# The last block's second FF product by Strassen's seven products, in a Trainium2 kernel of a hybrid decoder layer

## The chip, the cores and the metric

One core of one Trainium2 chip. The metric is the device time of one execution, in microseconds. The kernel before takes 2714.3 us, the median of three runs (2713.03 to 2716.78).

## What is computed

One decoder layer for 2048 tokens of width 1024, in float32, cut here to what matters:

```python
z = rms_norm(x, norm_mix_g) @ w_in
mixed = concatenate([rwkv7_heads(z), window_attention(z)])
x = x + mixed @ w_out
u = rms_norm(x, norm_mlp_g)
x = x + square(relu(u @ w_ff_up)) @ w_ff_down        # 1024 -> 4096 -> 1024
e = rms_norm(p @ ple_proj, ple_norm_g)
x = x + e * sigmoid(x @ ple_gate)
return rms_norm(x, final_norm_g)
```

The change concerns `square(relu(u @ w_ff_up)) @ w_ff_down` for the last 512 tokens.

## The kernel before

**Blocks and stages.** The tokens go in four blocks of 512 (TBK), b = 0 to 3. A block passes through `norm` and `proj` (input projection), `mix` (four tiles of 128 tokens, 26 steps each: the delta rule and the attention) and `fin` (output projection, norm, FF, the embedding branch ple and its gate, final norm). Each of the five engines runs the same `whole_program`: first the blocks' projections with the mixing of block 0 beside them, then `fin(b - 1)` beside the mixing of block b, where two hand-written lists of places (`BESIDE_PROJ`, `BESIDE_FIN`) say after how many pieces of `fin` each mixing step stands in the engine's order. `fin(3)`, the last, runs alone. The order on an engine is fixed; engines wait for each other by semaphores, one count for each step named in the lists `FIN_PE`, `FIN_ACT`, `FIN_DVE` (class `Marks`). The queues of SP (all loads of weights) and GpSimd run in order too; GpSimd has no work.

**Precision.** A product a x w is made of three matmuls in fp32r: a_hi x w_hi, a_hi x w_lo, a_lo x w_hi, where hi is the number rounded to fp32r and lo the rest.

**Weights.** They pass in chunks of 128 x 1024 numbers (512 KB), numbered over the whole kernel. SP loads chunk n into `raw`, slot n % 4, once the low part of chunk n - 4 is written (`load_weights`, L377). ScalarE copies it into `w_hi` (`high`, L980), VectorE writes `w_lo` (`low`, L1292) and TensorE begins the chunk when that is done. `w_hi` and `w_lo` have two slots: chunk n + 1 is split while chunk n is multiplied.

**FF.** The hidden width of 4096 goes in four groups (g, HG = 4) of 1024. The up product of a group has eight steps i, one chunk of 24 matmuls each (`up_half`, L860 to L864), whose result of 128 hidden features x 512 tokens lies in one of PSUM's banks 0 to 3. VectorE makes relu and the token's scale into `tmp` (L1636), ScalarE squares it twice, as h_hi (L1172) and exactly (L1173), VectorE writes the rest h_lo (L1639). In block 3's program ScalarE and VectorE split the next weight chunk ahead of each step's relu. The down product of a group has two column halves n of four chunks c, in which four token tiles j are multiplied in banks 0 to 3 (`by_tokens`, L818, L821, L822), 24 matmuls a chunk; VectorE adds the four banks into x (L1655) after each half: 8 adds a group. In the last group, eight transposes of the p block (L907, "pt") stand between up and down in banks 0 and 1; ScalarE and VectorE take them as p_hi (L1178) and p_lo (L1645), and the group's first down matmuls wait for p_lo. The row of scales comes from TensorE to `stage_f` by ScalarE (L1170, inv_row); after the FF `e_copy` (L1195) writes the ple product to the same memory `e`.

```python
for k in range(2):                                             # by_tokens, token tile j
    mm = T.matmul(ps[:, j, :], ah, wh, start=(first and k == 0), stop=False)
    T.matmul(ps[:, j, :], ah, wl, start=False, stop=False)
    mm = T.matmul(ps[:, j, :], al, wh, start=False, stop=(final and k == 1))
```

Of the kernel before, what the change touches and what calls it, by code (L numbers as in the profile page):

```python
# [13 lines left out]
P = 128  # L14
# [7 lines left out]
ZT = 20  # L22
# [84 lines left out]
class Marks:  # L107


    def __init__(self, sem, steps):  # L110
        self.sem, self.steps, self.seen = sem, steps, 0
        self.place = {s: i for i, s in enumerate(steps)}
        assert len(self.place) == len(steps)

    def mark(self, step):
        assert self.steps[self.seen % len(self.steps)] == step, (self.steps[self.seen % len(self.steps)], step)
        self.seen += 1
        return self.sem

    def done(self, n, step):  # L120
        return self.sem, n * len(self.steps) + self.place[step] + 1
# [58 lines left out]
FIN_CHUNKS = 8 + HG * 16 + 2 + 8  # L180

# [56 lines left out]
def finish_layer(nc, x, p, mixT, out, params, consts, ple_g, final_g, w_out, w_up, w_down, w_ple, w_gate, first_block):  # L238
# [3 lines left out]
    with ExitStack() as ctx:  # L242
# [20 lines left out]

        ones = sb("ones", [P, P])
# [30 lines left out]
        attT = pp[:, 0, :, :]  # L295

# [35 lines left out]
        fin_pe, fin_act, fin_dve = Marks(sem("fin_pe"), FIN_PE), Marks(sem("fin_act"), FIN_ACT), Marks(sem("fin_dve"), FIN_DVE)  # L332
# [7 lines left out]
        LAST_CHUNK = fin_chunk(BLOCKS - 1, FIN_CHUNKS - 1)  # L340

        def weights(n):
# [4 lines left out]
            i = (n - BLOCKS * ZT) % FIN_CHUNKS  # L347
# [4 lines left out]
            if i < HG * 16:  # L352
                g, i = divmod(i, 16)
# [4 lines left out]
            i -= HG * 16  # L358
# [6 lines left out]
        with nc.Block() as block:  # L365
            @block.sync
            def _(sp):
                def load_weights(n):
                    if n > LAST_CHUNK:
                        return  # L370
                    if n >= 4:
                        sp.wait_ge(w_lo_done, n - 3)
                    parts = weights(n)
# [94 lines left out]
                def fin(b):  # L468
# [25 lines left out]
                    for g in range(HG):  # L494
                        for i in range(8):
                            chunk()
                            yield
                            yield
                        if g == HG - 1:
# [41 lines left out]
            def _(pe):  # L541
# [3 lines left out]
                def begin(n):  # L545
# [5 lines left out]
                    return n % 2  # L551
# [252 lines left out]
                def fin(b):  # L804
# [8 lines left out]
                    def by_tokens(s, hi, lo, k0, j, first, final, name, opens):  # L813

                        for k in range(2):
                            ah, al = (a[:, k0 + k, j * P:(j + 1) * P] for a in (hi, lo))
                            wh, wl = (w[:, s, k * 512:(k + 1) * 512] for w in (w_hi, w_lo))
# [15 lines left out]

                    for n in range(2):
# [19 lines left out]
                    def up_half(s, g, i, half):  # L854
                        bank = up_bank(g, i)
                        for k in range(4 * half, 4 * half + 4):
                            if g == 0 and i == 0:
                                done(fin_dve, f"lo{k if half else 3}")
                            wh, wl = (w[:, s, k * P:(k + 1) * P] for w in (w_hi, w_lo))
# [8 lines left out]
                    for r in range(4):  # L868
# [12 lines left out]
                        yield  # L881
                    for g in range(HG):
                        for i in range(8):
# [3 lines left out]
                            elif g and i < 4:  # L887
                                done(fin_dve, f"down_add{g - 1}_1_{i}")
                            elif i >= 4:
                                done(fin_dve, f"relu{g}_{i - 4}")  # L890
# [10 lines left out]
                        if g == HG - 1:  # L901
                            pe.wait_ge(p_in, 16 * (b + 1))
                            done(fin_dve, f"relu{g}_4")
                            done(fin_dve, f"relu{g}_5")
# [878 lines left out]
```

## Time and profile before

| | us |
|---|---|
| median of three runs | 2714.3 |
| lowest and highest run | 2713.03, 2716.78 |
| span of the profiled execution, first to last instruction | 2710.3 |
| TensorE, VectorE, ScalarE, GpSimd busy in it | 2670.7, 1761.8, 1098.8, 0.2 |
| FF of the last block (about 2295 to 2640), TensorE busy | 342.5 of 345 |

The profiled execution's own device time was not kept apart from its span; beside the median of the runs the span is 4.0 us shorter. PE is TensorE's matmul, PEld its weight load, DVE VectorE, ACT ScalarE, POOL GpSimd, SP the queue that issues the loads. L1292 is line 1292 of the kernel. "Idle before" is the time that the engine stood idle just ahead of the instruction, and what ended it. Matmuls are pipelined: their durations overlap, so their starts say more than their lengths.

### The profile page before, as it was taken

Reading aid. Unit: us, or ns where it says so; the run is one execution under the profiler, and the core shown is the slowest. Engines: PE = TensorE matmul, PEld = TensorE weight load, DVE = VectorE, ACT = ScalarE, POOL = GpSimd, SP = SyncE. Lnnn points to the kernel's source line nnn. Section 1 sums busy time; section 2 is a strip of 40 time slices with the busy share of each in tenths; the row PEclk is TensorE's granted clock in tenths of the full one; section 3 lists DMA queues with packets and bytes.
Section 4 is the critical chain, followed back from the end, with each engine's and each line's share of the span. In section 5 each row is a group of like instructions: output and inputs, shape, how many; then the busy total and the mean of one; then the engine's idle time right before and its main releaser. Section 6 shows DMA issues by size and latency. Waiting matters only on the chain.

```text
span 2710.3 us, 57626 instructions
## 1 busy us (share of the span) xinstructions
PE 2670.7 (99%) x25202; PEld 2164.3 (80%) x25202; DVE 1761.8 (65%) x3037; ACT 1098.8 (41%) x1862; POOL 0.2 (0%) x4
## 2 busy tenths in 40 slices
PE   8999999999999999999999999999999999999998
PEld 6877787787878878878788888787878888888876
DVE  5477887857767674776776756867767565344435
ACT  4354444345333433653344325543434254233225
POOL 0000000000000000000000000000000000000000
PEclk9999999999999999999999999999999999999999
DMA  6564544463333334342332334433332244333332
GB/s 198 152 175 137 154 133 123 130 209 95 93 95 115 90 103 130 132 134 83 109 110 87 107 102 145 149 91 107 94 96 83 90 136 156 101 97 98 93 101 78
DMA packets 376199, 319.16 MB, mean 118 GB/s; under 512 B 48747, under 2 KB 328460, under 8 KB 375948
## 3 DMA queue, kind: packets, MB, share of 16 engines
q1 hardware_dynamic: 372272, 312.63, 38.4%
q8 instruction: 199, 3.26, 0.5%
q10 hardware_dynamic: 3676, 2.84, 0.4%
q14 instruction: 52, 0.43, 0.0%
HBM read 277.65 MB, written 38.14 MB: 117 GB/s over the span
## 4 chain that ended last, share of the span: by engine, by line
PE 79%; ACT 1%; DVE 1%; issue 0%; ACTq 0%
PE ps L818 14%; PE ps L821 13%; PE ps L822 13%; PE ps L860 9%; PE ps L864 9%; PE ps L863 9%; PE ps L703 2%; PE ps L675 1%; PE ps L831 1%; PE ps L774 1%; PE ps L622 1%; PE ps L591 1%; PE ps L614 1%; PE ps L595 1%; PE ps L594 1%; PE ps L628 1%
## 5 line engine op out<-in xcount | busy, mean ns | idle before, releaser
L1292 DVE TENSOR_TENSOR w_lo<-wraw_f,w_hi 128x1024 fp32r<-128x1024 f32 x408 | 497.5, 1219 | 345.8 <-ACT w_hi L980 344.5
L980 ACT ACTIVATE w_hi<-wraw_f 128x1024 fp32r<-128x1024 f32 x408 | 430.2, 1054 | 593.2 <-PE ps L818 504.6
L818 PE MATMUL ps<-w_hi,h_hi 128*128 128x512 f32 x1280 | 509.4, 398 | 3.1 <-DVE act_lo L1645 3.1
L821 PE MATMUL ps<-w_lo,h_hi 128*128 128x512 f32 x1280 | 499.1, 390 | 0.0
L822 PE MATMUL ps<-w_hi,h_lo 128*128 128x512 f32 x1280 | 499.0, 390 | 0.0
L860 PE MATMUL ps<-act_hi,w_hi 128*128 128x512 f32 x1024 | 412.6, 403 | 1.5 <-DVE w_lo L1292 1.4
L864 PE MATMUL ps<-act_hi,w_lo 128*128 128x512 f32 x1024 | 399.4, 390 | 0.0
L863 PE MATMUL ps<-act_lo,w_hi 128*128 128x512 f32 x1024 | 399.3, 390 | 0.0
L1172 ACT ACTIVATE h_hi<-tmp 128x512 fp32r<-128x512 f32 x128 | 80.9, 632 | 511.3 <-DVE tmp L1636 511.3
L818 PEld LDWEIGHTS ps<-w_hi,h_hi 128*128 128x128 f32 x1280 | 240.2, 188 | 58.1 <-issue 8.8
L822 PEld LDWEIGHTS ps<-w_hi,h_lo 128*128 128x128 f32 x1280 | 240.3, 188 | 51.7
L821 PEld LDWEIGHTS ps<-w_lo,h_hi 128*128 128x128 f32 x1280 | 240.5, 188 | 47.0
L860 PEld LDWEIGHTS ps<-act_hi,w_hi 128*128 128x128 f32 x1024 | 192.0, 188 | 47.1 <-issue 4.1
L864 PEld LDWEIGHTS ps<-act_hi,w_lo 128*128 128x128 f32 x1024 | 192.2, 188 | 41.6
L863 PEld LDWEIGHTS ps<-act_lo,w_hi 128*128 128x128 f32 x1024 | 192.4, 188 | 36.3
L1639 DVE TENSOR_TENSOR h_lo<-tmp,h_hi 128x512 fp32r<-128x512 f32 x128 | 88.7, 693 | 156.0 <-ACT tmp L1173 156.0
L1636 DVE SCALAR_TENSOR_TENSOR tmp<-ps,stage_f 128x512 f32<-128x512 f32 x128 | 88.3, 690 | 122.2 <-PE ps L864 119.5
L591 PE MATMUL ps<-act_hi,w_hi 128*128 128x512 f32 x320 | 129.5, 405 | 4.8 <-DVE w_lo L1292 4.4
L591 PE MATMUL ps<-h_hi,w_hi 128*128 128x512 f32 x320 | 128.6, 402 | 0.5 <-DVE h_lo L1303 0.5
L818 PE MATMUL ps<-w_hi,act_hi 128*128 128x512 f32 x320 | 126.3, 395 | 0.1
L595 PE MATMUL ps<-act_hi,w_lo 128*128 128x512 f32 x320 | 125.6, 392 | 0.0
L594 PE MATMUL ps<-act_lo,w_hi 128*128 128x512 f32 x320 | 125.4, 392 | 0.0
(227 smaller groups left out, 3731.1 us busy)
## 6 DMA issues: line engine op xcount, KB each, us to landing
wraw_f<-in_w_ff_up SPq DMA_DIRECT2D x256, 256.0 KB, 3.3
wraw_f<-in_w_ff_down SPq DMA_DIRECT2D x128, 512.0 KB, 4.0
wraw_f<-in_w_in SPq DMA_DIRECT2D x80, 512.0 KB, 4.4
zT<-tmp SPq DMA_DIRECT2D x80, 256.0 KB, 2.1
wraw_f<-in_w_out SPq DMA_DIRECT2D x32, 512.0 KB, 4.2
wraw_f<-in_w_gate SPq DMA_DIRECT2D x32, 512.0 KB, 3.9
zs<-zT SPq DMA_DIRECT2D x16, 896.0 KB, 5.8
h_lo<-mixT SPq DMA_DIRECT2D x4, 2048.0 KB, 8.8
```

What stands on the lines that cost most here:

```text
L591: mm = T.matmul(dst, wh, hi[:, k, :], start=(k == 0), stop=False)
L594: T.matmul(dst, wh, lo[:, k, :], start=False, stop=False)
L595: mm = T.matmul(dst, wl, hi[:, k, :], start=False, stop=(k == DK - 1))
L818: mm = T.matmul(ps[:, j, :], ah, wh, start=(first and k == 0), stop=False)
L821: T.matmul(ps[:, j, :], ah, wl, start=False, stop=False)
L822: mm = T.matmul(ps[:, j, :], al, wh, start=False, stop=(final and k == 1))
L860: mm = T.matmul(ps[:, bank, :], wh, act_hi[:, k, :], start=(k == 0), stop=False)
L863: T.matmul(ps[:, bank, :], wh, act_lo[:, k, :], start=False, stop=False)
L864: mm = T.matmul(ps[:, bank, :], wl, act_hi[:, k, :], start=False, stop=(k == DK - 1))
L980: S.activation(w_hi[:, n % 2, :], raw[:, n % 4, :], ACT.Copy).then_inc(w_hi_done, 1)
L1292: V.tensor_tensor(w_lo[:, n % 2, :], raw[:, n % 4, :], w_hi[:, n % 2, :].bitcast(F32), ALU.subtract).then_inc(w_lo_done, 1)
L1639: V.tensor_tensor(h_lo[:, i, :], tmp[:, i % 2, :], h_hi[:, i, :].bitcast(F32), ALU.subtract).then_inc(fin_dve.mark(f"h_lo{g}_{i}"), 1)
```

## The change

In `fin(3)` alone, the down product of each group, h (512 tokens x 1024) by w (1024 x 1024), is cut in 2 x 2 parts and made of seven products instead of eight (Strassen's, in Winograd's form). A token half is 256 wide, a feature half 512, a column half 512.

- **Factors of h.** A11, A12 and A22 are parts of h; S1 to S4 are sums of parts. The up steps go in the order 0, 4, 1, 5, 2, 6, 3, 7, so that both feature halves of a pair stand near each other. VectorE and ScalarE make of each step: for i below 4, A11 hi and lo, S3 exact, hi, lo; for i of 4 and more, A12 and A22 hi and lo, S1, S2, S4 exact, hi, lo. In this part the next weight chunk's split stands behind the step's relu and squares (ScalarE) and behind its relu (VectorE), and a step's low parts of sums stand in the following step.
- **Factors of w.** Three products take parts of w_down; four take sums, which GpSimd makes once, during the FF of block 0: 16 rounds (group, feature tile) of a load of four parts (1 MB) into `e`, four subtractions of 128 x 512, and a store (1 MB) to `w_sums` in DRAM, each waiting for the one before. ScalarE's first e_copy of block 0 waits for the last store, and SP's load of the first product's chunk too.
- **Products.** In the order P1, P5, P6, P3, P7, P2, P4, each two chunks of 12 matmuls, two token tiles in two banks (4 and 5, 2 and 3, or 6 and 7). P6, P7 and P4 go on in the banks of P1, P3 in those of P5, once VectorE has added these into x: 14 adds a group. P1 waits for A11's last low part, P5 for S1's, the first up steps of the next group for the add of P3.
- **Slots.** From the last block's FF on, `w_hi` and `w_lo` have six slots, four of them in memory of the mixing, and chunk n + 4 is split beside chunk n (two chunks each beside the first three). The block has 106 chunks where there were 82.
- **Last group.** Products don't wait for p_lo. SP's load of ple_g stands behind the fifth product chunk. `end_sum`'s scratch output lies in other memory.

The core of the diff:

```diff
+PRODUCTS = ("P1", "P5", "P6", "P3", "P7", "P2", "P4")
+INTO = {"P1": (0, 0), "P5": (1, 1), "P6": (0, 1), "P3": (0, 1), "P7": (1, 1), "P2": (0, 0), "P4": (1, 0)}
+UP_ORDER = (0, 4, 1, 5, 2, 6, 3, 7)
+LEAD, SLOTS = 4, 6
...
+        def split_beside(n):
+            if n < FIRST_AHEAD:
+                return [n + 1]
+            return {0: [n + 1, n + 2], 1: [n + 2, n + 3], 2: [n + 3, n + 4]}.get(n - FIRST_AHEAD, [n + LEAD])
...
                     if n >= 4:
                         sp.wait_ge(w_lo_done, n - 3)
+                    if n == FIRST_AHEAD + 8:
+                        sp.wait_ge(sums_stored, 16 * 4 * HG)
...
+                    def products(g):
+                        added_before = {"P6": "P1", "P7": "P6", "P4": "P7", "P3": "P5"}
+                        for n, p in enumerate(PRODUCTS):
+                            goes_on = p in added_before
+                            if goes_on:
+                                done(fin_dve, adds_of(g, added_before[p])[-1])
+                            elif p == "P5":
+                                done(fin_dve, f"relu{g}_{UP_ORDER[7]}")
+                            elif g:
+                                done(fin_dve, adds_of(g - 1, {"P1": "P4", "P2": "P2"}[p])[-1])
+                            if p == "P1":
+                                done(fin_dve, f"loA{g}_3")
+                            for half in range(2):
+                                s = chunk()
+                                for k in range(2):
+                                    kt = 2 * half + k
+                                    if p == "P5":
+                                        done(fin_dve, f"loS{g}_{4 + kt}")
+                                    if p == "P3" and kt == 0:
+                                        done(fin_dve, f"loS4{g}_7")
...
+                                    for j in range(2):
...
+                                        mm = T.matmul(dst, ah, wh, start=(not goes_on and kt == 0), stop=False, skip_group_check=goes_on)
...
+                                        T.matmul(dst, ah, wl, start=False, stop=False, skip_group_check=goes_on)
+                                        mm = T.matmul(dst, al, wh, start=False, stop=(kt == 3), skip_group_check=goes_on)
...
+                    def ff_last(g, s):                                  # ScalarE
+                        i = UP_ORDER[s]
+                        kt, h = i % 4, tmp[:, s % 2, :]
+                        done(fin_dve, f"relu{g}_{i}")
+                        if i < 4:
+                            S.activation(comb(0, "A11", kt), h[:, 0:256], ACT.Square)...
+                            S.activation(ex[:, kt, :], h, ACT.Square)...
+                        else:
+                            S.activation(two_comb(0, "A12", kt), h.rearrange("p (c t) -> p c t", c=2), ACT.Square)...
+                            S.activation(h, h, ACT.Square)...
+                        if s < 7:
+                            chunk()
+                        if i < 4:
+                            done(fin_dve, f"S3{g}_{i}")
+                            S.activation(comb(0, "S3", kt), ex[:, kt, 0:256], ACT.Copy)...
+                            return
+                        done(fin_dve, f"S2{g}_{i}")
+                        S.activation(two_comb(0, "S2", kt), ex[:, kt, :].rearrange("p (c t) -> p c t", c=2), ACT.Copy)...
+                        done(fin_dve, f"S4{g}_{i}")
+                        S.activation(comb(0, "S4", kt), h[:, 0:256], ACT.Copy)...
...
+                            if b == 0 and n == 0 and j == 0:             # ScalarE, ahead of e_copy0_0
+                                act.wait_ge(sums_stored, 16 * 4 * HG)
...
+            @block.gpsimd
+            def _(pool):
...
+                pool.wait_ge(*fin_act.done(0, "inv_row"))
+                for g in range(HG):
+                    for kt in range(4):
+                        n = 4 * g + kt
+                        if n:
+                            pool.wait_ge(sums_stored, 16 * n)
+                        pool.dma_start(four_parts, w_down[4 * g:4 * g + 4][:, :, kt, :].rearrange("q p f -> p q f")).then_inc(parts_in, 16)
+                        pool.wait_ge(parts_in, 16 * (n + 1))
+                        for i, (to, left, right) in enumerate(sums):
+                            if i:
+                                pool.wait_ge(part_sum, 4 * n + i)
+                            G.tensor_tensor(to, left, right, ALU.subtract).then_inc(part_sum, 1)
+                        pool.wait_ge(part_sum, 4 * n + 4)
+                        pool.dma_start(w_sums[4 * g:4 * g + 4, :, kt, :].rearrange("q p f -> p q f"), four_parts).then_inc(sums_stored, 16)
...
+                    def ff_last(g, s):                                  # VectorE
...
+                        V.scalar_tensor_tensor(h, ps[:, up_bank(g, s), :], 0.0, inv_row, ALU.max, ALU.mult)...
+                        if s < 7:
+                            chunk()
+                        if s:
+                            low_of_sums(g, s - 1)
+                        done(fin_act, f"hA{g}_{i}")
+                        done(fin_act, f"exact{g}_{i}")
+                        if i < 4:
+                            V.tensor_tensor(comb(1, "A11", kt), early, comb(0, "A11", kt).bitcast(F32), ALU.subtract)...
+                            done(fin_dve, f"loA{g}_{i}")
+                            V.tensor_tensor(early, early, late, ALU.subtract)...
+                            return
+                        V.tensor_tensor(two_comb(1, "A12", kt), ...)
+                        done(fin_dve, f"loS{g}_{kt}")
+                        V.tensor_tensor(late, h[:, 256:512], late, ALU.add)...
+                        V.tensor_tensor(early, h[:, 256:512], early, ALU.subtract)...
+                        done(fin_dve, f"S2{g}_{i}")
+                        V.tensor_tensor(h[:, 0:256], h[:, 0:256], early, ALU.subtract)...
...
+                    def down_last(g):
+                        for n in range(len(PRODUCTS)):
+                            if n:
+                                add_product(g, PRODUCTS[n - 1])
+                            chunk()
+                            chunk()
+                        add_product(g, PRODUCTS[-1])
```

## Rows read from the trace of the kernel before

**Rows 1.** The page, part 1: busy us, share of the span and instructions
```profile
PE 2670.7 (99%) x25202; PEld 2164.3 (80%) x25202; DVE 1761.8 (65%) x3037; ACT 1098.8 (41%) x1862; POOL 0.2 (0%) x4
```

**Rows 2.** Table of stretches: span, busy us (instructions) by engine, PEclk, DMA share, GB/s
```profile
0.00:100.00 100.00, 88.57 (x398) 73.13 (x399) 56.17 (x108) 44.13 (x69) 0.20 (x4) 0.98 0.63 187
640.00:1072.00 432.00, 431.20 (x4935) 346.90 (x4934) 295.10 (x522) 157.88 (x273) 0.00 (x0) 1.00 0.35 100
2295.00:2640.00 345.00, 342.49 (x1516) 283.48 (x1515) 142.56 (x160) 100.89 (x129) 0.00 (x0) 1.00 0.32 99
```

**Rows 3.** Timeline, one up step of the last block: start us, us, instruction, idle before
```profile
2396.39 0.69 DVE L1636 SCALAR_TENSOR_TENSOR tmp<-ps,stage_f 128x512 f32<-128x512 f32 x1 [1.35 <-PE ps L864]
2396.42 0.39 PE L863 MATMUL ps<-act_lo,w_hi 128*128 128x512 f32 x1
...
2396.65 0.39 PE L864 MATMUL ps<-act_hi,w_lo 128*128 128x512 f32 x1
...
2397.12 0.63 ACT L1172 ACTIVATE h_hi<-tmp 128x512 fp32r<-128x512 f32 x1 [3.34 <-DVE tmp L1636]
...
2397.66 0.61 ACT L1173 ACTIVATE tmp<-tmp 128x512 f32<-128x512 f32 x1
...
2398.18 1.04 ACT L980 ACTIVATE w_hi<-wraw_f 128x1024 fp32r<-128x1024 f32 x1
...
2399.25 1.23 DVE L1292 TENSOR_TENSOR w_lo<-wraw_f,w_hi 128x1024 fp32r<-128x1024 f32 x1 [0.26 <-ACT w_hi L980]
...
2401.83 0.69 DVE L1636 SCALAR_TENSOR_TENSOR tmp<-ps,stage_f 128x512 f32<-128x512 f32 x1 [1.36 <-PE ps L864]
```

**Rows 4.** Groups of instructions, 2295 to 2640 us: busy us, mean ns, idle before
```profile
L818 PE MATMUL ps<-w_hi,h_hi 128*128 128x512 f32 x256 | 99.7, 389 | 2.5 <-DVE act_lo L1645 2.5
...
L907 PE MATMUL ps<-con,line 128*128 128x128 f32 x8 | 1.0, 272 | 0.0
```

**Rows 5.** Timeline of VectorE: neighbouring starts, in mixing, a down step and the end
```profile
846.70 0.43 DVE L1505 TENSOR_TENSOR bm<-bm,knorm 128x256 f32<-128x256 f32 x1
847.04 0.88 DVE L1368 SCALAR_TENSOR_TENSOR work<-ps,bias 128x320 f32<-128x320 f32 x2
...
2435.85 1.23 DVE L1292 TENSOR_TENSOR w_lo<-wraw_f,w_hi 128x1024 fp32r<-128x1024 f32 x1 [4.21 <-ACT w_hi L980]
2437.00 1.28 DVE L1655 TENSOR_TENSOR x<-ps,x 128x512 f32<-128x512 f32 x2
...
2695.04 0.69 DVE L1695 TENSOR_TENSOR stage_f<-tmp,stage_f 128x512 f32<-128x512 f32 x1 [4.75 <-ACT tmp L1227]
2695.77 0.69 DVE L1697 TENSOR_TENSOR stage_f<-stage_f,x 128x512 f32<-128x512 f32 x1
2696.41 0.69 DVE L1695 TENSOR_TENSOR stage_f<-tmp,stage_f 128x512 f32<-128x512 f32 x1
```

**Rows 6.** Groups of instructions of the whole span, a 256-wide ScalarE one
```profile
L1105 ACT ACTIVATE work<-ps 128x256 f32<-128x256 f32 x16 | 6.1, 384 | 54.7 <-PE ps L692 54.7
```

**Rows 7.** Timeline of VectorE, first and third relu of the last block's FF
```profile
2293.63 0.69 DVE L1636 SCALAR_TENSOR_TENSOR tmp<-ps,stage_f 128x512 f32<-128x512 f32 x1 [1.17 <-ACT stage_f L1170]
...
2303.91 0.69 DVE L1636 SCALAR_TENSOR_TENSOR tmp<-ps,stage_f 128x512 f32<-128x512 f32 x1 [1.36 <-PE ps L864]
```

**Rows 8.** ScalarE's inv_row (L1170) and e_copy (L1195): first and last start
```profile
L1170 ACT ACTIVATE stage_f<-ps x4: 597/597/599, 640.6 to 2293.0; 128x512 f32<-128x512 f32 x4
...
L1195 ACT ACTIVATE stage_f<-ps x32: 591/597/603, 1072.4 to 2650.8; 128x512 f32<-128x512 f32 x32
```

**Rows 9.** The page, part 6, DMA issues: count, KB each, us to landing
```profile
wraw_f<-in_w_ff_down SPq DMA_DIRECT2D x128, 512.0 KB, 4.0
...
zs<-zT SPq DMA_DIRECT2D x16, 896.0 KB, 5.8
```

**Rows 10.** Timeline of block 0: sa0 on VectorE and the matmul that reads it
```profile
789.69 0.85 DVE L1401 TENSOR_TENSOR work<-ps,knorm 64x256 f32<-64x256 f32 x2
...
791.09 0.39 PE L751 MATMUL ps<-work,beta_t 64*64 64x64 f32 x6
```

More of the change, by code:

```diff
@@ L107, with __init__ @@
 class Marks:
[L110 removed]
+    def __init__(self, sem, steps, of_last=None, last=0):
         self.sem, self.steps, self.seen = sem, steps, 0
@@ L113, in __init__ @@
         assert len(self.place) == len(steps)
+        self.of_last, self.before_last = of_last, last * len(steps)
+        self.place_last = {s: i for i, s in enumerate(of_last or ())}
+        assert len(self.place_last) == len(of_last or ())
     def mark(self, step):
-        assert self.steps[self.seen % len(self.steps)] == step, (self.steps[self.seen % len(self.steps)], step)
+        if self.of_last and self.seen >= self.before_last:
+            expected = self.of_last[self.seen - self.before_last]
+        else:
+            expected = self.steps[self.seen % len(self.steps)]
+        assert expected == step, (expected, step)
         self.seen += 1
@@ L120, in done @@
     def done(self, n, step):
+        if self.of_last and n * len(self.steps) >= self.before_last:
+            return self.sem, self.before_last + self.place_last[step] + 1
         return self.sem, n * len(self.steps) + self.place[step] + 1
@@ L498, in fin @@
                             yield
+                        if b == BLOCKS - 1:
+                            for q in range(PIECES):
+                                chunk()
+                                if g == HG - 1 and q == 4:
+                                    sp.wait_ge(*fin_pe.done(b, "pt"))
+                                    load_gain(ple_g)
+                            continue
                         if g == HG - 1:
@@ L1628, in fin, with add_product @@
                     V.reciprocal(stat[:, 1, :], stat[:, 5, :]).then_inc(fin_dve.mark("inv"), 1)
+                    def add_product(g, p):
+                        n = PRODUCTS.index(p)
+                        if n or g:
+                            done(fin_dve, adds_of(g if n else g - 1, PRODUCTS[n - 1])[-1])
+                        r, c = INTO[p]
+                        for j in range(2):
+                            done(fin_pe, f"{p}_{g}_{j}")
+                            of_x = xr[:, 2 * r + j, half(c)]
+                            V.tensor_tensor(of_x, ps[:, bank_of[p] + j, :], of_x, ALU.add).then_inc(fin_dve.mark(f"add{p}_{g}_{j}"), 1)
@@ L1632, in fin @@
                             yield
+                            if b == BLOCKS - 1:
+                                if g == 0 and i == 0:
+                                    done(fin_act, "inv_row")
+                                ff_last(g, i)
+                                continue
                             if g == 0 and i == 0:
```

200 lines of the change are left out of this document (172 added, 28 removed).

## The prediction, made before the changed kernel was run

> **What bounds the kernel now.** Read the page's first part first [rows 1]: TensorE is busy 99% of the span, VectorE 65%, ScalarE 41%, and GpSimd does nothing. Then the table of stretches [rows 2]. Its second row is the stretch that the change rewrites, the FF of the last block, with no mixing beside it: TensorE 342.5 of 345 us at a granted clock of 1.00 (the 2.4 GHz level), VectorE 143, ScalarE 101, transfers at 0.32. So a matmul taken out there shortens the kernel, until a queue of another engine becomes the longer one.
>
> What is a matmul worth? The groups give it 389 ns [rows 4], but matmuls overlap: two neighbours start 0.23 us apart, and the relu of one up step follows that of the step before by 2401.83 - 2396.39 = 5.44 us for 24 matmuls [rows 3]. The price is 5.44 / 24 = 0.2267 us, not 0.389.
>
> **What is removed.** A group's down product takes 8 chunks of 24 matmuls, 192. Seven products take 7 x 2 token tiles x 4 feature tiles x 3 = 168. Four groups save 96 x 0.2267 = **21.8 us**. Also removed is the wait of 2.5 us in which TensorE stands before the last group's first down matmul until act_lo (p_lo) is written [rows 4]: the new products open in banks 4 and 5 and need no p_lo. Together **-24.3 us**.
>
> **What is added in the last block's FF.** Take one up step, time counted from the start of its relu. Before [rows 3]: ScalarE's square at 0.73, the exact square at 1.27, the weight copy at 1.79, VectorE's w_lo at 2.86; it is free 2.6 us before the next up step ends. After the change VectorE has in order: relu, w_lo (which waits for ScalarE's two squares and copy), the low parts of the step before, loA, then the sums. Nothing overtakes w_lo, so all of it lies in one chain. Starts on VectorE lie nearer than durations: a 1024-wide w_lo holds the queue 1.15 us, an independent 512-wide operation some 0.62 (between 0.64 and the 0.59 that a merged pair of 1.28 leaves), a dependent one 0.73, a 256-wide one 0.34; a dependent 256-wide one I take as its duration of 0.43 and the same 0.04 of passing on, less rounding 0.46 [rows 5].
> - Step with i of 4 or more: 2.86 + 1.15 (w_lo) + 0.34 (low part of S3) + 0.62 (loA) + 0.34 (S1) + 0.46 (S2, on which S4 waits) + 0.34 (S4) = 6.1 us.
> - Step with i below 4: the first square is 256 wide, so w_lo starts some 0.2 earlier, 2.65 (a 256-wide ScalarE operation takes 0.38 where a 512-wide one takes 0.63 [rows 3, 6]). 2.65 + 1.15 + 0.62 + 0.34 (low parts of S2/S1 and S4) + 0.46 (loA, on which S3 waits) + 0.34 = 5.55 us.
>
> TensorE offers an up step every 5.44 us. So the two queues, though each is idle half the time, fall behind it. In groups 1 to 3 the first step has no low parts before it and is in time, and the second relu starts at 2 x 5.44 + 0.2 = 11.08. Then 17.2, 22.7, 28.8, 34.4, and the seventh (i = 3) at 40.5. Its loA ends 2.65 + 1.15 + 0.62 + 0.34 + 0.43 = 5.2 later, at 45.7. P1 waits for it, and TensorE is through its eight up steps at 43.5: a wait of 2.2 us. In group 0 the first two steps carry a second weight chunk each (+1.15): from the relu at 2293.63 [rows 7], 5.75 + 7.25 + 5.55 + 6.1 + 5.55 + 6.1 bring the seventh to 2329.9 and loA_3 to 2335.1, where TensorE is through at 2303.9 - 0.2 + 5 x 5.44 = 2330.9: 4.2 us. In group 3 the eight transposes of p (1.0 us [rows 4]) run in the wait: 1.2 are left. Sum 4.2 + 2.2 + 2.2 + 1.2 = **+9.8 us**. It is sensitive: five steps hold 28 such VectorE operations, so 0.05 us more for each is 1.4 us a group and 5.6 in all, and as much shorter brings it to some 4.
>
> Priced at nothing, each with its cover:
> - The later waits of the products. P5 needs loS of the last up step, some 51 on that clock; its last factor is used after 45.7 + 5.4 + 4. P6 needs the add of P1 into x, which VectorE makes behind loS4 and two w_lo (2.3 us): done near 55, P6 is due at 56.6. The cover is 1.5 us, less than that in group 3, where two p_lo stand ahead. From P3 on VectorE has two w_lo and two adds (2.3 + 1.3 = 3.6 us, adds at 0.69 as other 512-wide ones [rows 5]) for each 5.44 us. If the cover is gone, P6 is late by the difference, up to 1 us a group.
> - 14 adds for 8 per group: in those gaps.
> - 24 more chunks: ScalarE and VectorE have the time. In the products TensorE eats 512 KB in 12 x 0.2267 = 2.72 us, 193 GB/s; SP's load of chunk n waits for the w_lo of n - 4. Landing takes 4.0 us [rows 9], a split is due two products, 10.9 us, after its load at the earliest, less 2.3 for the split: 8.6 us of room. SP's only new wait, for the sums, comes over 1,000 us after they are stored. The load of ple_g, moved in SP's queue behind its p transpose, waits as before.
> - ScalarE makes two copies (one more) ahead of hi6 and hi7 before the FF: 1 us, and hi7 waits 1.35 us for its transpose anyway.
> - The end_sum scratch is other memory.
>
> **What is added in block 0: GpSimd.** 16 rounds of a 1 MB load, four 128 x 512 subtractions in a chain, a 1 MB store, each waiting for the last. Neither the operation nor its queue is in this trace. A load of 896 KB lands in 5.8 us [rows 9], so two transfers are some 13 us. The subtraction is bounded below by VectorE's 0.69 [rows 5]; above, nothing here bounds it but the window: from inv_row at 640.6 to the first e_copy at 1072.4, 432 us [rows 8], or 27 us a round, which 3.4 us a subtraction would fill. I take 1.3, about twice VectorE's, 18 us a round and 290 in all, ended 140 us early: ScalarE's new wait before e_copy0_0 costs nothing. Traffic rises by some 110 GB/s over the 100 of that stretch, which makes 210, near the 187 that the first 100 us carry [rows 2], for buffers that are filled two chunks and more ahead.
>
> What can cost is VectorE held up. In that stretch TensorE stands idle 0.8 of 432 us, VectorE is busy 295 [rows 2], and mixing steps hang on it closely: sa0 is written at 790.54 and the matmul that reads it starts at 791.09, 0.55 us of slack [rows 10]. No row shows a GpSimd operation beside a VectorE one. The cost lies between 0 (they don't meet) and 64 x 1.3 = 83 us (each delays TensorE by its length). A gain is excluded, as nothing in block 0 is taken out. The slack rows lie between, and I take 64 x 0.06 = **+4 us**: one subtraction in four meets such a step, and a quarter of a us passes the slack. This is the least certain term.
>
> The Trainium skill (SBUF — State Buffer, section on the two separate sides) says that a VectorE instruction with two SBUF inputs and a GpSimd one that reads SBUF exclude each other for a whole instruction. By it the holding up is real; without it this term would be 0, and the sum 2700.
>
> **Sum.** 2714.3 - 24.3 + 9.8 + 4 = **2703.8 us**. The profiled span is 2710.3, 4.0 under the median of the three runs (2713.0 to 2716.8); all terms are differences within the span, whose frame I leave alone: a span of 2699.8.
>
> **Rivals.**
> 1. *The whole saving arrives.* If VectorE and ScalarE's chain is shorter than I add it up (waits met early, shorter starts), P1 waits 0 to 5 us and GpSimd costs nothing: 2690 to 2695. For it: each engine is half idle. Against: the chain runs through both. 0.12.
> 2. *The chain is longer.* 0.1 us for each operation (second waits, the strided halves) gives 9.8 + 11.2 = 21 us of waits for P1: 2715. 0.12, no difference.
> 3. *GpSimd holds VectorE back* in block 0. Place: w_lo, h_lo and the two-input steps of mixing, while a subtraction runs. From 64 x 0.31 = 20 us (14.5 that are left of the gain, and 5.4) it makes the kernel slower; at half a us each, 32 us, 2732. For it: slack of half a us; against: VectorE is idle a third of the time and later steps give the delay back. 0.14 for slower; 0.1 for a cost between 9 and 20, no difference. By the lock rule of the Trainium skill (SBUF — State Buffer, the two separate sides) this is where it ends if enough meetings fall on tight steps.
> 4. *Weights late in the products*: landings of 10 us instead of 4.0 would add some 1.5 us for each of seven products, four times: +40 us, slower. 0.03.
>
> The forecast's own case has 0.49. With 0.2%, 5.4 us, as about what a measurement of this kernel can tell: faster is the forecast's case but for 0.02, and rival 1, 0.59. No difference: 0.02 + 0.12 + 0.1 = 0.24. Slower: 0.17. The range runs from the low end of rival 1 (2695) to a GpSimd cost of 20 us (2720).
>
> **What would show it.** In the changed profile's last FF: starts of neighbouring matmuls still 0.23 us apart, 1,440 of them, no wait before the last group's products for p_lo; relus about 5.8 us apart late in each group; TensorE idle 2 to 4 us before each P1, released by VectorE's loA; P5 to P4 without waits. In 640 to 950: POOL busy 80 us or so in 16 bursts, TensorE idle up to 5 us more. Wrong if P1 starts on time, if TensorE waits for w_lo or transfers in the products, if its idle time in the first 1,000 us grows by 10 or more, or if e_copy0_0 waits for the sums.

## The result, and the profile after

The changed kernel takes 2724.56 us, the median of seven runs (2720.17 to 2737.07), against 2714.19 of the kernel before in the same runs: ratio 1.0044 as recorded over the runs, interval 1.0035 to 1.0053 (the two medians alone give 1.0038). It is slower by 10 us at the medians, where 2703.8 was forecast. In the experiments a few executions ran at a far lower clock (one of e2, 4434.6 us; of the kernel before beside them one each of 2950.0 and 8034.1 us): they are in the medians given, but in no ratio. The profiled execution is the longest of the seven (2737.07, span 2735.1), so its losses are larger than the median's; the profiles of the experiments below agree on where they lie.

The page of the changed kernel: the span, part 1, GpSimd's row of part 2, its queue of part 3 and its two transfers of part 6.

```profile
span 2735.1 us, 57875 instructions
...
PE 2672.6 (98%) x25106; PEld 2160.5 (79%) x25106; DVE 1874.7 (69%) x3197; ACT 1141.1 (42%) x1934; POOL 123.3 (5%) x100
...
POOL 0000000002433400000000000000000000000000
...
q0 software_dynamic: 8704, 33.56, 3.4%
...
stage_f<-in_w_ff_down POOLq DMA_DIRECT2D x16, 1024.0 KB, 7.2
w_sums<-stage_f POOLq DMA_DIRECT2D x16, 1024.0 KB, 5.3
```

TensorE's work has hardly changed and there are 96 fewer matmuls (25106 where 25202 were), yet the span is 25 us longer. GpSimd is at work in five slices only, those of block 0's FF, which answers to [rows 8]. Its transfers land 7.2 us (a load) and 5.3 us (a store) after their issue, and the last store is issued 148 us before e_copy0_0, which waits for nothing. In the changed kernel the line of inv_row is L1361 and that of e_copy L1391; the views of these two lines (first and last start in the third column), the second one also for the last block alone:

```profile
L1361 ACT ACTIVATE stage_f<-ps x4: 597/597/599, 641.7 to 2324.6; 128x512 f32<-128x512 f32 x4
...
L1391 ACT ACTIVATE stage_f<-ps x32: 590/597/601, 1104.1 to 2673.2; 128x512 f32<-128x512 f32 x32
...
L1391 ACT ACTIVATE stage_f<-ps x8: 590/597/599, 2663.2 to 2673.2; 128x512 f32<-128x512 f32 x8
```

and the same of the kernel before for the last block's e_copy, the other three starts being in [rows 8]:

```profile
L1195 ACT ACTIVATE stage_f<-ps x8: 591/597/598, 2640.8 to 2650.8; 128x512 f32<-128x512 f32 x8
```

These starts cut both profiled executions into five parts (differences of the rows, us; the same was done with every kernel below):

| kernel | to first inv_row | block 0: inv_row to e_copy | to last inv_row | last FF: inv_row to e_copy | to the end |
|---|---|---|---|---|---|
| before | 640.6 | 431.8 | 1220.6 | 347.8 | 69.5 |
| changed | 641.7 | 462.4 | 1220.5 | 338.6 | 71.9 |
| e1, no GpSimd | 642.0 | 431.8 | 1220.5 | 338.6 | 71.5 |
| e2, transfers only | 643.1 | 432.0 | 1220.4 | 338.6 | 71.7 |
| e3, subtractions only | 639.9 | 455.0 | 1220.5 | 338.6 | 71.8 |
| e7, memsets | 641.6 | 431.8 | 1220.4 | 338.4 | 71.6 |
| e8, half subtractions | 642.1 | 438.7 | 1220.5 | 338.6 | 71.6 |
| e4, split first | 639.4 | 452.6 | 1220.5 | 329.3 | 73.2 |
| e5, order and tail | 639.2 | 447.5 | 1220.5 | 323.2 | 69.5 |
| e6, sums on VectorE | 641.3 | 431.8 | 1220.5 | 323.3 | 69.6 |

Read the second line against the first: +1.1, **+30.6**, -0.1, **-9.2**, +2.4, together the 24.8 us between the two spans. The last FF gained; block 0 lost three times as much.

**Block 0.** The table of stretches (span, busy us by engine, PEclk, DMA share, GB/s) of the changed kernel, for its block 0 and its last FF, which answers to [rows 2]:

```profile
640.00:1104.00 464.00, 447.14 (x4941) 356.19 (x4940) 333.59 (x525) 158.85 (x275) 123.10 (x96) 0.97 0.53 166
2324.00:2663.00 339.00, 330.54 (x1436) 272.15 (x1435) 223.09 (x326) 147.46 (x205) 0.00 (x0) 0.98 0.45 143
```

TensorE stands idle 464.0 - 447.1 = 16.9 us, where it stood 0.8, and its granted clock is 0.97, not 1.00. A mean of 0.97 over 464 us is 6% of them, 28 us, at 1.2 instead of 2.4 GHz, and costs half of that, some 14 us. Slices of 10 us show where: the clock is below 1.00 from 710 to 770 and from 850 to 890 us (0.82 to 0.96), and they add up to 13.6. 16.1 us more of standing and some 14 of half clock make about 30 of the 30.6. TensorE's waits in that stretch (us in total, times, longest):

```profile
PE ps L748 <- DVE work L1671: 4.3, 2, 2.7
PE ps L981 <- DVE w_lo L1509: 3.7, 5, 1.3
PE ps L823 <- DVE yb L1719: 2.5, 1, 2.5
PE ps L938 <- DVE w_lo L1509: 2.1, 1, 2.1
```

These are the four largest groups, 12.6 of the 16.9 us, all for VectorE (of the rest, 1.7 us are for ScalarE). Why is VectorE late? The groups of VectorE from 640 to 960 (busy us, mean ns), first of the kernel before:

```profile
L1292 DVE TENSOR_TENSOR w_lo<-wraw_f,w_hi 128x1024 fp32r<-128x1024 f32 x47 | 57.3, 1218 | 16.3 <-ACT w_hi L980 16.1
L1639 DVE TENSOR_TENSOR h_lo<-tmp,h_hi 128x512 fp32r<-128x512 f32 x24 | 16.6, 693 | 29.2 <-ACT tmp L1173 29.2
L1636 DVE SCALAR_TENSOR_TENSOR tmp<-ps,stage_f 128x512 f32<-128x512 f32 x24 | 16.5, 688 | 20.1 <-PE ps L864 19.6 <-ACT stage_f L1170 0.3
...
L1478 DVE TENSOR_TENSOR work<-bm,knorm 32x256 f32<-32x256 f32 x12 | 5.0, 415 | 0.2
```

then of the changed kernel, with GpSimd's group of the whole span:

```profile
L1509 DVE TENSOR_TENSOR w_lo<-wraw_f,w_hi 128x1024 fp32r<-128x1024 f32 x43 | 59.9, 1393 | 12.8 <-ACT w_hi L1147 12.6
L1923 DVE TENSOR_TENSOR h_lo<-tmp,h_hi 128x512 fp32r<-128x512 f32 x24 | 21.3, 887 | 29.3 <-ACT tmp L1367 29.3
L1920 DVE SCALAR_TENSOR_TENSOR tmp<-ps,stage_f 128x512 f32<-128x512 f32 x24 | 16.4, 683 | 14.0 <-PE ps L985 13.5 <-ACT stage_f L1361 0.3
...
L1695 DVE TENSOR_TENSOR work<-bm,knorm 32x256 f32<-32x256 f32 x8 | 10.4, 1300 | 0.1
...
L1496 POOL TENSOR_TENSOR stage_f<-stage_f 128x512 f32<-128x512 f32 x64 | 98.6, 1540 | 110.8 <-DMA stage_f<-in_w_ff_down 107.0
```

The relu (L1636, now L1920) reads PSUM and one tile of SBUF: 688 and 683 ns, untouched. w_lo, h_lo and the small masking step L1478 (now L1695) read two tiles of SBUF: 1218 became 1393, 693 became 887, and 415 became **1300** ns. GpSimd's subtraction takes 1.54 us. The timeline shows one meeting: a burst of GpSimd's four subtractions, and VectorE's row in it, four instructions in a row.

```profile
746.62 6.37 POOL L1496 TENSOR_TENSOR stage_f<-stage_f 128x512 f32<-128x512 f32 x4 [4.85 <-DMA stage_f<-in_w_ff_down]
...
748.92 4.79 DVE L1695 TENSOR_TENSOR work<-bm,knorm 32x256 f32<-32x256 f32 x4
```

The four of the kernel before:

```profile
841.68 1.71 DVE L1478 TENSOR_TENSOR work<-bm,knorm 32x256 f32<-32x256 f32 x4
```

4.79 us where they took 1.71, as if each of them but one waited for a subtraction to end (3 x 1.54 is 4.6). Over the whole of block 0 (first inv_row to first e_copy), VectorE's 523 instructions are busy 332.8 us where the same number took 294.9 before: 37.9 us longer, of which TensorE pays only what passes the slack.

**The last FF.** TensorE's waits from 2323 us on, and the timeline of VectorE at the end of group 0's up steps (the relus of the sixth and seventh up step, w_lo, loA_3) with the matmul that opens P1:

```profile
PE ps L1028 <- DVE s_lo L1887: 8.5, 4, 3.8
PE ps L938 <- ACT tmp L1423: 2.2, 1, 2.2
```

```profile
2355.26 0.68 DVE L1879 SCALAR_TENSOR_TENSOR tmp<-ps,stage_f 128x512 f32<-128x512 f32 x1
...
2361.32 0.68 DVE L1879 SCALAR_TENSOR_TENSOR tmp<-ps,stage_f 128x512 f32<-128x512 f32 x1
2363.95 1.22 DVE L1509 TENSOR_TENSOR w_lo<-wraw_f,w_hi 128x1024 fp32r<-128x1024 f32 x1 [1.95 <-ACT w_hi L1147]
...
2366.03 0.42 DVE L1887 TENSOR_TENSOR s_lo<-ex,s_hi 128x256 fp32r<-128x256 f32 x1
...
2366.50 0.79 PE L1028 MATMUL ps<-w_hi,s_hi 128*128 128x512 f32 x1 [3.81 <-DVE s_lo L1887]
```

These two relus are 6.06 us apart (across the steps of group 0: 5.72, 7.19, 5.51, 6.06, 5.52, 6.06), w_lo and its wait for ScalarE lie between them, and P1 starts right behind loA_3 (2366.03, 0.42 long), 3.81 us late. The four waits for P1 are 3.8, 1.8, 1.8 and 1.0 us, 8.5 together; 9.8 were forecast. The first three are followed by a lower granted clock, the fourth isn't (table of stretches, from the start of P1 on, groups 0 and 3):

```profile
2366.00:2383.00 17.00, 16.50 (x62) 13.38 (x63) 13.84 (x21) 8.54 (x11) 0.00 (x0) 0.83 0.48 155
2630.00:2645.00 15.00, 15.00 (x68) 12.43 (x67) 13.09 (x15) 8.07 (x8) 0.00 (x0) 1.00 0.76 237
```

The clock is 0.83 behind the 3.8 us gap, 0.95 and 0.94 behind the two of 1.8, and 1.00 behind the one of 1.0. The mean of 0.98 over 339 us costs 6.8 by the same reckoning; shorter stretches add up to 6.5. So 347.8 - 24.3 + 8.5 + 6.8 = 338.8; the table has 338.6.

**The tail.** The queue of SP, ScalarE's weight copy, and TensorE's second gate half, which waits for the sigmoids (L1423):

```profile
2692.15 0.33 SPq L645 DMA_DIRECT2D line<-in_final_g  x1
...
2692.52 0.43 SPq L490 DMA_DIRECT2D wraw_f<-in_w_gate  x1
...
2697.94 1.06 ACT L1147 ACTIVATE w_hi<-wraw_f 128x1024 fp32r<-128x1024 f32 x1 [11.71 <-DMA wraw_f<-in_w_gate]
...
2701.05 0.47 PE L938 MATMUL ps<-w_hi,act_hi 128*128 128x512 f32 x1 [2.23 <-ACT tmp L1423]
```

SP loads final_g after a wait for e_norm3, and behind that comes the last gate chunk. With a lead of four, ScalarE splits this chunk ahead of its sigmoids and stands 11.7 us for it; TensorE waits 2.2 us for the banks that the sigmoids free.

### The profile page after: what moved, and what is told of

Its sections match the earlier page's. It is cut to its first block, busy times and chain, and to the rows that moved or that the text cites. A ratio compares the mean times of both kernels' runs of the same rounds, so it can differ in the third digit from the quotient of the medians.

```text
span 2735.1 us, 57875 instructions
## 1 busy us (share of the span) xinstructions
PE 2672.6 (98%) x25106; PEld 2160.5 (79%) x25106; DVE 1874.7 (69%) x3197; ACT 1141.1 (42%) x1934; POOL 123.3 (5%) x100
## 4 chain that ended last, share of the span: by engine, by line
PE 68%; DVE 7%; ACT 3%; issue 2%; DMA 0%; ACTq 0%; SPq 0%
PE ps L938 11%; PE ps L941 10%; PE ps L942 10%; PE ps L981 7%; PE ps L984 6%; PE ps L985 6%; PE ps L1028 2%; PE ps L1031 2%; PE ps L1032 2%; ACT w_hi L1147 1%; PE ps L823 1%; DVE w_lo L1509 1%; PE ps L951 1%; PE ps L795 1%; PE ps L894 1%
## 5 line engine op out<-in xcount | busy, mean ns | idle before, releaser
L1509 DVE TENSOR_TENSOR w_lo<-wraw_f,w_hi 128x1024 fp32r<-128x1024 f32 x432 | 531.4, 1236 | 290.2 <-ACT w_hi L1147 288.8
L1147 ACT ACTIVATE w_hi<-wraw_f 128x1024 fp32r<-128x1024 f32 x432 | 454.2, 1054 | 537.0 <-PE ps L938 376.2
L938 PE MATMUL ps<-w_hi,h_hi 128*128 128x512 f32 x1024 | 414.4, 405 | 2.7 <-DVE w_lo L1509 2.1
L941 PE MATMUL ps<-w_lo,h_hi 128*128 128x512 f32 x1024 | 403.7, 394 | 0.0
L942 PE MATMUL ps<-w_hi,h_lo 128*128 128x512 f32 x1024 | 403.1, 394 | 0.0
L938 PEld LDWEIGHTS ps<-w_hi,h_hi 128*128 128x128 f32 x1024 | 194.7, 190 | 48.6 <-issue 6.1
L1366 ACT ACTIVATE h_hi<-tmp 128x512 fp32r<-128x512 f32 x96 | 60.7, 632 | 408.2 <-DVE tmp L1920 408.2
L942 PEld LDWEIGHTS ps<-w_hi,h_lo 128*128 128x128 f32 x1024 | 194.8, 190 | 42.7
L941 PEld LDWEIGHTS ps<-w_lo,h_hi 128*128 128x128 f32 x1024 | 195.2, 191 | 37.8
L714 PE MATMUL ps<-h_lo,w_hi 128*128 128x512 f32 x320 | 125.2, 391 | 0.0
```

The source lines that it names most:

```text
L714: T.matmul(dst, wh, lo[:, k, :], start=False, stop=False)
L1147: S.activation(of_high(slot_of(n)), raw[:, n % 4, :], ACT.Copy).then_inc(w_hi_done, 1)
L1509: V.tensor_tensor(of_low(s), raw[:, n % 4, :], of_high(s).bitcast(F32), ALU.subtract).then_inc(w_lo_done, 1)
```

## The experiments

Two theories for block 0. **Port**: a GpSimd subtraction and a VectorE operation with two SBUF inputs exclude each other. **Transfers**: GpSimd's 33 MB delay the loads. For the last FF: **chain** (the order of w_lo makes P1 late) against **work** (VectorE has too much to do in all). e1 to e4 ran on one chip, whose kernel before took 2713.5 us, and e5 to e8 on another, 2714.4 us; the changed kernel's 2724.6 comes from the runs with 2714.2. Each ratio is to the kernel before of its own chip. The kernels e1, e2, e3 and e7 don't compute the layer: they multiply by plain parts of w_down where sums belong.

**e1_no_gpsimd.**

```diff
-            @block.gpsimd
...
-                    return [w_down[...][:, part, :] if p in of_weights else w_sums[4 * g + of_sums[p], :, part, :]]
+                    return [w_down[...][:, part, :] if p in of_weights else w_down[4 * g + of_sums[p]][:, part, :]]
```

> GpSimd's 16 rounds and the waits for them are left out; the four products that take sums of weights take plain parts of w_down in the same number and size of chunks (so their factor of w is not the sum). Port theory and transfer theory alike: block 0 (first inv_row to first e_copy) returns from 462 us to 432, the last block's FF stays as in the changed kernel (P1 waits 8.5 us in sum). Sum: 2714.2 - 24.3 + 8.5 + 2.4 of the late gate weights = 2701, and up to 2708 if the three falls of the clock in the last FF stay. If the loss sat in the last FF instead, it would stay near 2720.

2705.25 us, ratio 0.9969 (0.9956 to 0.9982). Block 0 is back at 431.8, the last FF unchanged at 338.6. So GpSimd's part costs 2724.6 - 2705.3 = 19 us at the medians (30.6 in the profiled execution), and the last block with its tail saves 8 of the 24.

**e2_transfers_only.**

```diff
-                            G.tensor_tensor(to, left, right, ALU.subtract).then_inc(part_sum, 1)
```

> GpSimd's 16 loads and 16 stores stay, its 64 subtractions are left out (w_sums holds plain parts). Port theory (subtractions and VectorE's operations with two SBUF inputs exclude each other): no lengthened VectorE operation, block 0 within 1 us of 432, time as e1 within 2 us, about 2701 to 2708. Rival (33 MB of extra transfers or their descriptors delay SP's loads): as the changed kernel, 2720 or more, with TensorE waiting in block 0.

2706.82 us, 0.9971 (0.9959 to 0.9982); block 0 432.0, at 176 GB/s between 640 and 1110 us where e1 has 105. VectorE's groups from 640 to 960:

```profile
L1504 DVE TENSOR_TENSOR w_lo<-wraw_f,w_hi 128x1024 fp32r<-128x1024 f32 x47 | 57.3, 1218 | 16.3 <-ACT w_hi L1147 16.0
```

as before the change. The transfers cost nothing that shows here; that theory falls.

**e3_subtractions_only.**

```diff
-                        pool.dma_start(four_parts, w_down[...]).then_inc(parts_in, 16)
...
-                        pool.dma_start(w_sums[...], four_parts).then_inc(sums_stored, 16)
```

> The 64 subtractions stay, one chain without pauses, all transfers of GpSimd are left out (the products take plain parts of w_down). Port theory: w_lo, h_lo and the two-input mixing steps are as long as in the changed kernel or longer while it runs, in some 100 us after 641; TensorE waits 10 to 20 us there and its clock falls; 2710 to 2725. Rival (transfers): 2701 to 2708, as e1.

2728.23 us, 1.0054 (1.0038 to 1.0070), 3 us over the expectation. Block 0 takes 455.0. The same groups:

```profile
L1503 DVE TENSOR_TENSOR w_lo<-wraw_f,w_hi 128x1024 fp32r<-128x1024 f32 x44 | 62.8, 1427 | 11.2 <-ACT w_hi L1147 10.9
L1917 DVE TENSOR_TENSOR h_lo<-tmp,h_hi 128x512 fp32r<-128x512 f32 x24 | 20.6, 857 | 29.3 <-ACT tmp L1367 29.3
...
L1638 DVE TENSOR_SCALAR work<-work,par,omka 128x128 f32<-128x128 f32 x12 | 7.5, 688 | 0.0
```

The last row has one tile of SBUF as input, with two scalars for each partition, and it is held too: 336 ns on average before. Four of these in a row took 5.32 us beside the subtractions, where four took 1.09 before. So the port theory, as worded above, is too narrow: operations with two SBUF inputs are not the only ones held.

The subtractions alone bring a loss as large as the whole one, at other places: here they stand in one row of 104 us.

**e7_memset.**

```diff
-                            G.tensor_tensor(to, left, right, ALU.subtract).then_inc(part_sum, 1)
+                            G.memset(to, 0.0).then_inc(part_sum, 1)
```

> As e3_subtractions_only, but GpSimd's 64 operations are memsets of 128 x 512, which write SBUF and read nothing (products take plain parts of w_down). If only a GpSimd operation that reads SBUF excludes VectorE's with two SBUF inputs: no lengthened VectorE operation, time as e1_no_gpsimd, 2705. If any GpSimd operation on SBUF excludes them: as long as its own duration each, 2708 or more, w_lo and h_lo lengthened in the stretch after 641.

2704.70 us, 0.9963 (0.9949 to 0.9976), block 0 431.8. The groups of VectorE, and GpSimd's:

```profile
L1503 DVE TENSOR_TENSOR w_lo<-wraw_f,w_hi 128x1024 fp32r<-128x1024 f32 x47 | 57.3, 1218 | 16.3 <-ACT w_hi L1147 16.1
L1917 DVE TENSOR_TENSOR h_lo<-tmp,h_hi 128x512 fp32r<-128x512 f32 x24 | 16.6, 692 | 29.3 <-ACT tmp L1367 29.3
...
L1492 POOL MEMSET stage_f<- 128x512 f32 x64 | 33.7, 526 | 645.4 <-ACT stage_f L1361 641.8
```

w_lo and h_lo don't move by more than 1 ns from the kernel before. The memsets stand in one row of 37 us (642.2 to 679.5), and the steps beside it are what counts: the 8 w_lo from 641 to 690 us take 1.19 to 1.23 us and the 7 h_lo 0.69 to 0.70, where the 12 w_lo beside the row of subtractions in e3 have a median of 2.10. The memset is also shorter than the subtraction, 0.53 us against 1.54, but it is there the whole time and no two-input step waits for it. One step did last longer beside it: a four-wide TENSOR_SCALAR (neg, L1595) took 0.35 us instead of 0.17, a single case that decides nothing.

**e8_half_subtractions.**

```diff
+                            for c in range(2):
+                                cols = slice(256 * c, 256 * c + 256)
-                            G.tensor_tensor(to, left, right, ALU.subtract).then_inc(part_sum, 1)
+                                G.tensor_tensor(to[:, cols], left[:, cols], right[:, cols], ALU.subtract).then_inc(part_sum, 1)
```

> The changed kernel with each subtraction cut into two of 256 columns (128 in all, the same sums). Port theory: one hold lasts half as long, VectorE's operations are lengthened by at most some 0.8 us at a time, more often; TensorE waits less since more holds stay inside the slack of half a us to 2 us: block 0 some 445 to 455 us instead of 462, 2710 to 2722. Rival (the loss goes with the total time that GpSimd computes): no change, 2724.

2711.47 us, 0.9990 (0.9980 to 0.9999): 13 us less than the changed kernel, with more GpSimd time, 113 us where it was 99.

```profile
L1511 DVE TENSOR_TENSOR w_lo<-wraw_f,w_hi 128x1024 fp32r<-128x1024 f32 x46 | 59.5, 1293 | 13.1 <-ACT w_hi L1147 12.8
...
L1498 POOL TENSOR_TENSOR stage_f<-stage_f 128x256 f32<-128x256 f32 x128 | 113.1, 918 | 110.9 <-DMA stage_f<-in_w_ff_down 110.9
```

Block 0 takes 438.7, less than the 445 to 455 expected, at a granted clock of 1.00; TensorE stands idle 6.4 us there. VectorE's 523 instructions are busy 314.5 us in it: 19.6 us longer than before the change, where the whole subtractions cost 37.9. So a hold half as long costs VectorE about half in sum, and TensorE less than half of its idle time, since more of what is left stays inside the slack. The rival (the loss goes with GpSimd's total time) falls.

**e4_split_first.**

```diff
+                        if s < 7:
+                            chunk()
                         done(fin_dve, f"relu{g}_{i}")                  # ScalarE; on VectorE ahead of done(fin_pe, f"up{g}_{i}")
...
-                        if s < 7:
-                            chunk()
```

> The changed kernel whole, but in the last block's up steps ScalarE and VectorE split the weight chunk ahead of the step's relu instead of behind it. Chain theory: the chain from relu to relu loses the copy and w_lo (some 2.2 us), relus follow 5.44 us apart, P1 waits under 1 us in each group, TensorE's clock does not fall in the last FF: 8 to 14 us less than the changed kernel, about 2711 to 2716. Rival (P1 waits for VectorE's total work, not its order): P1 still waits 2 us or more a group, no gain.

2714.19 us (2708.47 to 2720.08), 1.0000 (0.9990 to 1.0010), 10 us under the changed kernel; last FF 329.3. The size was right and half of the reason wrong. Relus are still 5.8 us apart on average (6.4 and 5.2 in turn), since ScalarE's copy now stands behind the squares of the step before, and w_lo with it in the same chain. What the edit changed is that no w_lo lies between the last relu and loA_3: three of the four waits go, group 0's stays at 4.2 us (the matmul that opens P1). The tail takes 73.2 us, 1.3 longer than in the changed kernel; why was not looked into.

```profile
2354.74 0.50 PE L1028 MATMUL ps<-w_hi,s_hi 128*128 128x512 f32 x1 [4.19 <-DVE s_lo L1887]
```

**e5_order_and_tail.**

```diff
                         V.scalar_tensor_tensor(h, ps[:, up_bank(g, s), :], 0.0, inv_row, ALU.max, ALU.mult)...
-                        if s < 7:
-                            chunk()
...
                         V.tensor_tensor(h[:, 0:256], h[:, 0:256], early, ALU.subtract)...   # and behind S3 for i < 4
+                        if s < 7:
+                            chunk()
...
-                        chunk()                                         # SP, gate, i = 4
+                        if i == 3 and b == BLOCKS - 1:                  # ahead of the wait for e_norm3
+                            chunk()
```

> The changed kernel with two orders altered. In the last block's up steps VectorE writes w_lo after the step's sums (ScalarE's copy stays behind the squares); SP loads the last gate chunk ahead of its wait for e_norm3. Chain theory: relu to relu has only the squares, loA and the sums in the chain (4.8 us, under 5.44), so P1 waits nowhere but for up to 2 us in group 0, the clock does not fall in the last FF, which takes 323.5 to 326 us where the changed kernel takes 338.6 and the kernel before 347.8; from e_copy to the end 69.5 us instead of 71.9. Block 0 as in the changed kernel. Sum some 16 us under the changed kernel, about 2708. Rival (P1 waits for VectorE's total work): last FF over 330.

2705.64 us (2699.39 to 2713.63), 0.9971 (0.9957 to 0.9985). Two relus with the w_lo between them, and the stretch of the last FF:

```profile
2328.95 0.69 DVE L1882 SCALAR_TENSOR_TENSOR tmp<-ps,stage_f 128x512 f32<-128x512 f32 x1 [0.50 <-PE ps L988]
...
2331.60 1.23 DVE L1512 TENSOR_TENSOR w_lo<-wraw_f,w_hi 128x1024 fp32r<-128x1024 f32 x1
2334.39 0.69 DVE L1882 SCALAR_TENSOR_TENSOR tmp<-ps,stage_f 128x512 f32<-128x512 f32 x1 [1.57 <-PE ps L988]
...
2300.00:2640.00 340.00, 339.91 (x1512) 281.37 (x1511) 233.04 (x335) 156.88 (x221) 0.00 (x0) 1.00 0.46 145
```

The relus follow 5.44 us apart, and w_lo stands behind the sums, and the relus wait 0.5 and 1.6 us for TensorE: that much is to spare. There is no wait for P1, not even the 2 us allowed for group 0, and no fall of the clock (1.00); the last FF takes 323.2, the end 69.5. 347.8 - 323.2 = 24.6: the whole saving of 24.3 us that the prediction priced arrives. The "work" theory falls. Block 0 still pays: 447.5, with TensorE idle for 14.3 us of it, and here the granted clock stays at 1.00, in every slice of 10 us.

**e6_vector_sums.**

```diff
-                            G.tensor_tensor(to, left, right, ALU.subtract).then_inc(part_sum, 1)     # GpSimd keeps the transfers
...
+                            half_sums(b, 8 * g + i)                    # VectorE, blocks 0 to 2, between relu and h_lo
                             done(fin_act, f"exact{g}_{i}")
                             V.tensor_tensor(h_lo[:, i, :], tmp[:, i % 2, :]...
...
+                        m, second = b * 11 + (step - 4) // 2, (step - 4) % 2
+                        for i in (2, 3) if second else (0, 1):
+                            V.tensor_tensor(*sums[i], ALU.subtract).then_inc(part_sum, 1)
```

> As e5_order_and_tail, and the sums of weights are made by VectorE: 32 half rounds (256 columns each, three buffers), two 256-wide subtractions in each up step of blocks 0, 1 and 2, between relu and h_lo, where VectorE stands 1.2 us waiting for ScalarE's exact square; GpSimd only issues the transfers. Port theory: no GpSimd operation touches SBUF, no VectorE operation is lengthened, block 0's FF takes 432 to 434 us, no fall of the clock there: 2714.2 - 24.3 + 0 to 5 = 2690 to 2695, faster than both kernels. Rival (any further work on VectorE in the mixing stage makes TensorE wait): 2700 or more, with waits in blocks 0 to 2.

**2688.76 us** (2688.61 to 2688.88), ratio 0.9903 (0.9887 to 0.9919): faster than both kernels, 25 us under the one before and 36 under the changed one. Its page's first part, and the stretch of block 0:

```profile
span 2686.5 us, 58004 instructions
...
PE 2649.9 (99%) x25106; PEld 2147.0 (80%) x25106; DVE 1889.4 (70%) x3325; ACT 1140.4 (42%) x1934; POOL 48.5 (2%) x68
...
640.00:1100.00 460.00, 459.04 (x5070) 369.60 (x5069) 327.35 (x588) 176.51 (x307) 16.69 (x22) 1.00 0.43 129
```

That is 1 us under the range expected. Block 0 takes 431.8 and the stretch with blocks 1 and 2 still 1220.5, as if nothing had been added. VectorE does 128 subtractions of some 0.42 us more, 44 of them in block 0, placed where it stood waiting for ScalarE. The four runs lie within 0.3 us of each other, those of e5 within 14. Probably the spread of the changed kernel comes from which VectorE steps GpSimd's subtractions happen to meet; no run tests that by itself.

## Why the prediction was wrong

- **TensorE's price and the saving: right.** 0.2267 us a matmul, 21.8 us for 96 and 2.5 for p_lo make 24.3: the last FF of e5 is 24.6 shorter than before, that of e6 24.5.
- **The chain of the last FF: right.** 9.8 us of waits for P1 were forecast, 8.5 measured (3.8 in group 0, 4.2 forecast), and each of the six distances between the relus of group 0 came within 0.06 us of the working. The later products never waited, nor did transfers.
- **A term left out:** three of the four waits for P1 are followed by stretches partly at 1.2 instead of 2.4 GHz, 6.8 us in sum. The prediction has no term for the clock, and gives no reason for leaving it out. Rows of the kernel before gave no warning: after its gap of 2.5 us the clock stayed at 1.00.
- **The step that failed: "+4 us" for GpSimd in block 0.** I took 64 x 0.06. Measured is 19 us at the medians, 0.30 each, and 30.6 or 0.48 in the profiled execution. The range of that step reached to 83, and rival 3 named the place and the threshold of 0.31 for "slower"; it had 0.14. At the medians 0.30 is just under this threshold: with the forecast's other terms (-24.3 + 9.8) it would have made the kernel 4.8 us slower, short of the 5.4 that the forecast counts as a difference. Two terms left out, the clock in the last FF (above) and the late gate chunk (below), put it beyond. Of the 21 us between forecast and measurement about 15 belong to the GpSimd term, and about 6, as e1 shows without GpSimd, to those two less the shorter waits for P1.
- **What was misjudged in it.** Two things. I let one subtraction in four meet a tight step with a quarter of a us beyond its slack, though with the chosen 1.3 us a single hold goes 0.8 past the 0.55 us of slack [rows 10], and four subtractions follow each other at once, so that a series of VectorE steps is held, as the 4.79 us show. And the granted clock was lower after such waits, which in the profiled execution nearly doubles them (16.9 us of standing, some 14 of half clock); in e5, with 14.3 us of standing in block 0, it stayed at 1.00, so this part does not come with every hold.
- The subtraction was put at 1.3 us and takes 1.54; a round takes some 19 us, and the last one ends in good time: e_copy0_0 waited for nothing, as forecast.
- **A queue misread, 2.4 us.** The prediction checked the move of ple_g's load and not final_g's, behind whose wait the last gate chunk stands, now due four chunks early.
- Sum by the measured terms for the profiled execution: 1.1 + 30.6 - 24.3 + 8.5 + 6.8 + 2.4 = 25.1 for the 24.8 between the spans.

The Trainium skill's rule (SBUF — State Buffer, the two separate sides) agrees with these traces: two-input VectorE operations beside subtractions are lengthened by up to about a whole subtraction (32 x 256: 415 to 1300 ns on average), the relu with one SBUF input is not (688, 683), and GpSimd operations that read nothing (e7) held no step with two SBUF inputs. The prediction named it and priced it too low.

## What to carry to other kernels

An idle engine is not free if its work holds up another one: here 64 GpSimd subtractions of 1.54 us beside a VectorE that works from SBUF cost 19 us at the medians, the holds and what they set off. Free time on the busy engine, at a place where it waits for another one anyway, was the better home for the same work. Where two half-idle engines hand a step back and forth, add up the chain from release to release against the pace of the bound engine, and put work that nobody waits for behind the work that somebody does.

## What the runs showed of the hardware that was not expected

- Four 32 x 256 VectorE operations in a row took 4.79 us instead of 1.71 beside a chain of GpSimd subtractions, and 512-wide memsets of GpSimd lengthened no step with two SBUF inputs (means of 1218 and 692 ns, as without GpSimd).
- A VectorE operation with one SBUF tile and scalars was held too: four TENSOR_SCALARs of 128 x 128 took 5.32 us in a row in e3 where four took 1.09 before (mean of all 12 there 688 ns, 336 before).
- Gaps of TensorE of 1.8 to 3.8 us ahead of P1 were followed by a lower granted clock (0.83 to 0.95) in three groups of the changed kernel, and the one of 1.0 us was not. e5, without these gaps, shows 1.00 in the last FF, and 1.00 over its block 0 too, where one of the gaps was 3.6 us long; the gap of 2.5 us in the kernel before left 1.00 [rows 2]. Which gap brings the clock down and which doesn't was not settled.
- Cutting GpSimd's subtractions in two raised their busy time from 99 to 113 us, halved what VectorE lost (37.9 to 19.6 us) and took 13 us off the kernel.
